# Ten buffers of weight halves at ten starting places instead of one

## The reference, cut to what matters

```python
def first_block(x, ...):
    for l in range(DEPTH):                       # DEPTH = 2
        x = x + 0.5 * swiglu(rms_norm(x, ffn1_norm[l]), ffn1_w_gate[l], ffn1_w_up[l], ffn1_w_down[l])
        x = x + hybrid_mixer(rms_norm(x, mix_norm[l]), w_in[l], ...)
        x = x + 0.5 * swiglu(rms_norm(x, ffn2_norm[l]), ffn2_w_gate[l], ffn2_w_up[l], ffn2_w_down[l])
    return rms_norm(x, final_norm)

def second_block(x, ...):
    for l in range(DEPTH):
        x = _layernorm(DEEPNORM_ALPHA * x + FFN_RES * _swiglu(x, ffn1_w_in[l], ffn1_w_out[l]), ...)
        mix = _hybrid_mixer(x, l, w_in[l], ...)
        x = _layernorm(DEEPNORM_ALPHA * x + mix, ln2_g[l], ln2_b[l])
        x = _layernorm(DEEPNORM_ALPHA * x + FFN_RES * _swiglu(x, ffn2_w_in[l], ffn2_w_out[l]), ...)
    return x
```

## Time and profile before

| | |
|---|---|
| median of 2 runs | 2814.77 us (2814.58 to 2814.96) |
| span of the profiled execution | 2812.3 us |
| PE busy | 2792.6 us, 99% |
| DVE busy | 1921.3 us, 68% |
| ACT busy | 1554.0 us, 55% |
| POOL busy | 241.5 us, 9% |
| mean share of the 16 DMA engines | about 50% |

### The profile page before, as it was taken

The page is one execution under the profiler, slowest core; times in us unless marked ns, Lnnn a source line. Parts: engine busy times, 40 slices in busy tenths (PEclk is TensorE's granted clock), DMA queues, the critical chain, the costliest instruction groups (busy, mean ns, idle before and its releaser), DMA issues.

```text
span 2812.3 us, 40293 instructions
## 1 busy us (share of the span) xinstructions
PE 2792.6 (99%) x15556; PEld 2396.6 (85%) x15556; DVE 1921.3 (68%) x3180; ACT 1554.0 (55%) x2718; POOL 241.5 (9%) x187
## 2 busy tenths in 40 slices
PE   9999999999999999999999999999999999999998
PEld 8889888888889888888888987888888888878887
DVE  6756676747655667756568777776566687777765
ACT  6545656545545656545456556455455465655553
POOL 0010011010010011010014100110100141001100
PEclk9999999999999999999999999999999999999999
DMA  6544445555544345555554344555555554445553
GB/s 242 191 171 158 149 156 182 193 185 190 195 167 152 139 172 194 199 190 195 195 193 179 136 163 159 210 194 182 199 189 195 183 187 153 158 156 184 209 185 135
DMA packets 75055, 503.82 MB, mean 179 GB/s; under 512 B 8784, under 2 KB 10480, under 8 KB 19184
## 3 DMA queue, kind: packets, MB, share of 16 engines
q1 hardware_dynamic: 74576, 501.07, 50.2%
q10 hardware_dynamic: 288, 0.17, 0.0%
HBM read 500.12 MB, written 1.08 MB: 178 GB/s over the span
## 4 chain that ended last, share of the span: by engine, by line
PE 93%; DVE 4%; POOL 2%; issue 1%; ACT 1%; DMA 0%; SPq 0%; DVEq 0%; ACTq 0%
PE ps L1544 45%; PE ps L1579 21%; PE ps L1585 11%; PE ps L1563 9%; PE ps L1606 3%; POOL wlo L2498 2%; DVE wlo L2038 1%; PE ps L1701 1%; PE ps L1699 1%; DVE conv L2327 1%; PE ps L1726 1%; PE ps L1716 0%; PE ps L1717 0%; PE ps L1718 0%; DVE ps L2144 0%
## 5 line engine op out<-in xcount | busy, mean ns | idle before, releaser
L1777 ACT ACTIVATE whi<-raw 128x1024 fp32r<-128x1024 f32 (+3 forms) x938 | 977.5, 1045 | 600.3 <-PE ps L1544 426.1
L2038 DVE TENSOR_TENSOR wlo<-raw,whi 128x1024 fp32r<-128x1024 f32 (+2 forms) x894 | 1084.1, 1220 | 219.9 <-ACT whi L1777 218.9
L1579 PE MATMUL ps<-xT_both,whi 128*128 128x512 f32 x2560 | 641.6, 393 | 0.0
L1544 PE MATMUL ps<-whi,xT_both 128*128 128x512 f32 (+2 forms) x2336 | 628.9, 391 | 2.6 <-DVE xT_both L2061 1.6
L1579 PEld LDWEIGHTS ps<-xT_both,whi 128*128 128x128 f32 x2560 | 461.1, 189 | 82.6
L1544 PEld LDWEIGHTS ps<-whi,xT_both 128*128 128x128 f32 x2336 | 425.5, 188 | 83.7 <-issue 9.3
L1585 PEld LDWEIGHTS ps<-xT_both,wlo 128*128 128x128 f32 x2560 | 349.3, 191 | 24.9
L1585 PE MATMUL ps<-xT_both,wlo 128*128 128x256 f32 x2560 | 357.1, 282 | 0.0
L1544 PE MATMUL ps<-wlo,xT_both 128*128 128x512 f32 (+2 forms) x1168 | 354.6, 385 | 0.3 <-DVE wlo L2038 0.3
L2118 DVE TENSOR_TENSOR h<-h,ps 128x256 f32<-128x256 f32 x320 | 127.0, 418 | 203.1 <-ACT h L1826 203.1
L1544 PEld LDWEIGHTS ps<-wlo,xT_both 128*128 128x128 f32 x1168 | 218.4, 188 | 43.7 <-DVE wlo L2038 1.4
(11 more groups left out here) (315 smaller groups left out, 2526.7 us busy)
## 6 DMA issues: line engine op xcount, KB each, us to landing
raw<-in_w SPq DMA_DIRECT2D x435, 1024.0 KB, 4.8
vr<-in_vrows SPq DMA_DIRECT2D x19, 512.0 KB, 5.6
raw<-in_w SPq DMA_DIRECT2D x12, 768.0 KB, 4.3
raw<-in_w SPq DMA_DIRECT2D x10, 896.0 KB, 4.5
sums<-scratch SPq DMA_DIRECT2D x8, 512.0 KB, 4.4
raw<-in_w SPq DMA_DIRECT2D x4, 832.0 KB, 4.4
raw<-in_w SPq DMA_DIRECT2D x4, 576.0 KB, 3.7
raw<-in_w SPq DMA_DIRECT2D x4, 512.0 KB, 6.9
```

Of the source, the lines that this page charges most:

```text
L1544: made = e.matmul(bank[:, 0:c1 - c0], xs[:, kt, sl], ws[:, j * w + c0:j * w + c1], start=kt == 0 and n == 0, stop=kt == job.nk - 1 and n == 2)
L1579: e.matmul(bank[:, :].rearrange("p (n x) -> p n x", n=2), hi[:, o:o + 128], job.xt.both[:, :, kt, :], start=kt == 0, stop=False, skip_grou ...
L1777: e.activation(out, raw, ACT.Copy).then_inc(*mark("hi", i))
L2038: e.tensor_tensor(out, raw, hi.bitcast(F32), sub).then_inc(*mark("lo", i))
```

## The change

Between the ten buffers stand fillers of 8 floats, 32 bytes, so that each begins 32 bytes further on within 256 bytes than the one ahead of it.

```diff
     many("raw", NRAW, [128, BLOCK])
-    many("whi", NHL, [128, PIECE], F32R)
     at_line = nc.sbuf_base % LINE
-    many("wlo", NHL, [128, PIECE], F32R)
+    for name, fills in (("whi", (0, 8, 8, 8, 8)), ("wlo", (8, 8, 8, 8, 8))):
+        m[name] = []
+        for i, n in enumerate(fills):
+            if n:
+                sbuf(f"{name}{i}_fill", [128, n])
+            m[name].append(sbuf(f"{name}{i}", [128, PIECE], F32R))
     many("x", 2, [128, D])
```

## The result

The changed kernel takes 2838.46 us (2 runs, 2838.17 to 2838.75) against 2814.77 us: ratio 1.0084, 95% interval 1.0055 to 1.0113. That is 23.7 us slower, clear of the interval and under 2%. The forecast, no change, did not come true; the time is close to the one that the slow rival's lighter case gave (2840 us).

The account below looks back on a forecast made before the run. The prediction took PE's matmul pace to bound the kernel. All price terms summed to 0 on the 2812.3 us span, plus 2.5 us around it: 2814.8 us, own range 2807 to 2822, 8-in-10 range 2803 to 2845.

Parts of the forecast that it names:

- slow rival: A weight stream from a place off the old grid costs one more fetch; 12% for slower up to 2%.
- lighter case: Five of ten buffers, at odd multiples of 32 bytes, pay: 2808 matmuls x 9 ns = 25 us, giving 2840 us.
- What bounds the kernel: Whole kernel: PE is busy 99% of the span, so the pace of the matmuls counts, not loads or halving.
- PE streaming weights ... I take 0: Matmuls streaming weights (L1544): a new place costs 0, bounds plus and minus 1.5 ns on 4,500 streams, 7 us.
- a need that both operands of a matmul begin at the same place: Possible reason for eight of ten buffers to pay: 4493 x 9 ns = 40 us, giving 2855 us.
- The scores read both operands ...: Price 0: Score matmuls at place 128 or 0 take 377 ns in the median either way, so stationary weight reads cost 0.
- so a little more would be hidden: Weights as stationary operand: their load runs beside the matmul ahead, so a small extra cost would not show.
- PE against the engines that write the halves: no collision: Down product: matmul pairs keep their pace whether ACT or DVE is working, so there is no collision to cure.
- ACT and DVE: Copies and subtractions: no address penalty to remove; 11 ns more per subtraction would cost the chain under 1 us.
- The other tensors: x, ident and stat move by 32 bytes: price 0; even 2 ns each would be a microsecond or two.
- The faster rival: Small rest in the up products is contention that spreading places removes: 10 to 15 us faster, 2802 us; 6%.
- 13.5 ns are fixed: Matmuls: of each 226.8 ns some 13.5 are fixed, leaving 0.014 of 2.79 us per up-product piece unexplained.

Follow-up runs that it names:

- ten160: Changed kernel with one 32-byte filler ahead of whi0 instead: all ten weight buffers at place 160, activations' halves at 128; 2846.89 us, ratio 1.0115.
- w32: Kernel before, with all ten weight buffers moved to place 32, activations' halves still at 128 (distance -96); 2859.00 us, ratio 1.0159.
- w192: Kernel before, with all ten weight buffers moved to place 192, activations' halves still at 128 (distance +64); 2808.10 us, ratio 0.9977.
- all160: Kernel before, with one 32-byte filler ahead of whi0 and the activations' halves lined up: weights and activations all at place 160; 2814.68 us, ratio 1.0001.
- x160: Kernel before, with a 32-byte filler behind wlo4: only x, xn, ident, cols, stat and phalf move by 32 bytes; 2815.01 us, ratio 1.0001.
- mix192: On top of w192, the activations' halves except xT also moved to place 192; 2803.45 us, ratio 0.9960.
- step64: Changed kernel with seven fillers of 64 bytes instead of the 32-byte ones, no odd multiple of 32; 2826.77 us, ratio 1.0043.
- one160: Kernel before, with only whi2 moved to place 160; the nine other weight buffers, x and the activations at 128; 2821.26 us, ratio 1.0024.

## Why the prediction was wrong in its forecast, step by step

**What bounds the kernel: right.** PE's pace sets the time, and the whole change of time is PE's.

**The ranges.** The 2838.5 us lie 16 us above the forecast's own range, 2807 to 2822. The wider range of 2803 to 2845 holds it, but only because it took in the lighter part of the slow rival; the mechanism that was forecast, a price of nothing, did not hold.

**"PE streaming weights ... I take 0": this is the step that failed.** It was 5.3 ns a matmul in the down products. The bound of 1.5 ns came from the `cq` matmuls, where half the streams begin 128 bytes off the stationary operand. They are 48 matmuls of 288 columns in short stretches. At distance +128 the 512-column streams do pay (59.94 us for 258, 5.5 ns each). The `cq` matmuls don't show it at any distance: their mean from start to start is 133.2 ns before, 133.2 in ten160, 133.2 in w32, where the 512-column streams are dearest, and 131.8 in w192. A price read off one width did not carry to another. The prediction also set the price per stream and per new place; the runs show that it belongs to the distance between the two operands, and to the matmuls just before, so the two unmoved buffers pay as well. For "a need that both operands of a matmul begin at the same place" the prediction had 4493 x 9 = 40 us, and 24 came: more streams pay than it counted, each pays less, and the 256-column ones give some back. That 2808 x 9 = 25 us fits the result is luck.

**"The scores read both operands ...: Price 0": wrong evidence.** L1699 and L1701 take both operands from one tensor, so the earlier trace rows compared distance 0 at place 128 with distance 0 at place 0. all160 says the same, that the absolute place costs nothing. The rows said nothing on distance, which is what the change alters.

**Weights as the stationary operand, "so a little more would be hidden": wrong, and in one part in the sign.** L1583, with `whi` stationary, grew by 6.1 us, while L1589 and L1567 fell by 6.5. The price is not hidden behind the matmul ahead; for 512 columns it is within 0.6 ns of the rows form's (the second table), and for 256 columns it can be a gain.

**"PE against the engines that write the halves: no collision": right.** ten160 and all160 have the writers alike and differ by 32 us; in ten160 the slow pace goes on while ACT is idle and while DVE is.

**ACT and DVE, "price 0": right.** DVE busy 1921.7 for 1921.3 us, ACT 1554.1 for 1554.0. The long subtractions stayed too (3324 ns at most for 3325, mean 1219 for 1220), so it is not the places that make them long. **The other tensors, "price 0": right**, x160.

**The rivals.** The slow one met the size, 2840 us against 2838.5, but its first reason (one more fetch from an odd multiple of 32) is refuted by all160. The half sentence in it, "a need that both operands of a matmul begin at the same place", named the right quantity, though no strict need: +64 costs 2.1 ns where the other distances cost 5.5 to 7.4. The slow rival as a whole, up to 2%, had been given 12%. The faster rival (6%) looked in the right place, the up products: w192 and mix192 do get below the former pace there, though the change as made doesn't. No run shows its cause, contention with the other engines. "13.5 ns are fixed" was a mistake of reading. The sum of an up product closed to 0.014 us because two misreadings nearly cancel: in the trace of before its 512-column matmuls take 230.0 ns, not 226.8, and its 256-column ones 119.1, not 120.2. In w192 these take 114.0.

**The stationary load and the running stream.** The Trainium skill, page "TensorE: Matmul & The Clock Gate", section "Step-by-step: what each phase is for", says that loading the next weights takes no read bandwidth from the running matmul. The runs here show that the two are not independent in pace: streams from the same addresses take 226.8 or 233.3 ns each by the place of the stationary operand (all160 and ten160, 58.51 and 60.20 us for 258). Whether it is the load that costs the stream its time, they don't show; where the sentence would have no price at all, the measurement decides.

**The changed kernel as a mixture.** Its `whi` have the distances 0, +32, +64, +96, +128, its `wlo` -96, -64, -32, 0, +32. The means of the table over these are 2832.3 and 2838.1 us; weighted two to one, as most products use `whi` twice and `wlo` once, 2834. Measured 2838.5. For step64 the same sum gives 2821.5 us, and 2826.8 were measured; for one160 it gives 2818.8, and 2821.3 were measured. The 2.5 to 5 us above the sum are of the kind that one160's timeline shows behind a change of distance; that they are all of this kind is not shown.

**What stays open.** Why the price has no simple order in the distance (for 512 columns +64 costs 2.1 ns and -64 costs 6.5 in the down products) and by what mechanism the two operands meet was not settled. That a stream and the load of the next stationary operand beside it hold each other up is a guess. One hint for it: in one160's up products the last 256-column matmul ahead of a `whi2` piece takes 118 or 119 ns from start to start, where the same matmuls take 119 to 121 in the trace of before (120 in nearly all). Its own two operands are at distance 0; only the operand loaded next is not. Distances under 32 bytes, and a different distance for `whi` and `wlo` alone, were not tried.

## What to carry to other kernels

Where matmuls bound a kernel, look at the distance modulo 256 bytes from the stationary operand to the streamed one, with its sign, not at either's own place, and measure it for each width of stream: here it was worth 51 us of 2814 between the best and the worst of eight, with no instruction changed. To price an edit, first ask which quantity it changes, and check that the rows taken as evidence vary in that quantity; two rows that differ only in something else say nothing. A part of the time that looks fixed in a profile is fixed only for the one arrangement it was read from.

## What the runs showed of the hardware that I had not expected

The pace of back-to-back matmuls of rounded float32 (fp32r) with 512 streamed columns depends on the distance of the operands: 226.8 ns at 0, 228.9 at +64, 232.3 at +128, 233.3 to 233.4 at +32, +96, -32 and -64, 234.2 at -96 (the first table's last column over 258; stream minus stationary). Which of the two tensors streams makes no difference to that, as the second table shows. A matmul's pace depends on those before it: after a piece at another distance three matmuls (228, 233 and 231 ns in one160) pass before the old pace is back, and behind 256-column matmuls at the same distance it takes five (in the trace of before). And 256-column matmuls, at 119 to 120 ns apparently at their floor before, sped up to 114.0 ns in w192, where their stream lies 64 bytes below the stationary operand: eight of 512 and eight of 256 columns took 2.77 us instead of 2.79 although the 512-column ones had become slower.
